# A raw memory projection with its norm applied at eviction, and head norms in column and row tiles of TensorE

## The reference

```python
def rmsnorm(x, g):
    y = x * lax.rsqrt(jnp.mean(x * x, axis=-1, keepdims=True) + EPS)
    return y * g

def memory_kv(mem, mem_norm_g, w_k, w_v, k_g):          # mem: 256 tokens x 2048
    mn = rmsnorm(mem, mem_norm_g)
    k = rmsnorm((mn @ w_k).reshape(B, N_MEM, MEM_H, MEM_HD), k_g)
    v = (mn @ w_v).reshape(B, N_MEM, MEM_H, MEM_HD)

# in layer(): xn = rmsnorm(x, norm1_g); one projection xn @ w_in gives the convolution, q, k, v, memory queries, gates
q = rmsnorm(qkv[:, :, :, 0], sw_q_g) * (SW_HD ** -0.5)   # 3 groups x 4 heads of 128
k = rmsnorm(qkv[:, :, :, 1], sw_k_g)
qm = rmsnorm(h_mq, mem_q_g) * (MEM_HD ** -0.5)           # 4 heads of 256
```

## Time and profile before

| | us |
|---|---|
| median of 3 runs | 3199.36 |
| lowest, highest | 3197.07, 3203.57 |
| the profiled execution | 3196.39 |
| its span (first to last instruction) | 3194.8 |
| PE busy in it | 3009.3 (94%) |
| DVE, ACT, POOL busy | 2007.6, 1361.9, 252.0 |

### The profile page before, as it was taken

One profiled execution on the slowest core, in us unless ns is written; L12 is line 12 of the kernel. 1 busy time (PEld: TensorE's weight loads), 2 busy tenths in 40 slices (PEclk: granted clock), 3 DMA queues, 4 the chain that ended last, 5 costly groups with the idle time before them and its releaser, 6 DMA issues.

```text
span 3194.8 us, 54045 instructions
## 1 busy us (share of the span) xinstructions
PE 3009.3 (94%) x21026; PEld 2777.8 (87%) x21026; DVE 2007.6 (63%) x2971; ACT 1361.9 (43%) x1825; POOL 252.0 (8%) x294
## 2 busy tenths in 40 slices
PE   5999998998868999999899999999999999999999
PEld 4899998866767998999899999999999887787777
DVE  4445886654323334643579986777774777787776
ACT  3343332344233333333334445777773443444444
POOL 1000001001000000100011101111100011011110
PEclk8999999989889999999999999999999999999999
DMA  4467778335654996867587878888887889999895
GB/s 163 164 224 279 275 266 207 116 114 182 232 208 159 392 369 255 310 241 260 193 296 272 280 280 289 309 331 307 328 315 265 310 331 334 335 339 331 329 329 186
DMA packets 227188, 854.95 MB, mean 268 GB/s; under 512 B 24768, under 2 KB 47312, under 8 KB 205104
## 3 DMA queue, kind: packets, MB, share of 16 engines
q1 hardware_dynamic: 182336, 563.68, 50.5%
q0 software_dynamic: 27088, 246.09, 21.6%
q10 hardware_dynamic: 17568, 42.48, 3.5%
HBM read 800.44 MB, written 139.26 MB: 294 GB/s over the span
## 4 chain that ended last, share of the span: by engine, by line
PE 75%; DMA 11%; DVE 8%; ACT 3%; issue 2%; DVEq 1%; SPq 0%; ACTq 0%; POOL 0%
PE ps L1546 19%; PE ps L1547 19%; PE ps L1548 19%; DMA raw<-in_v_rows 8%; PE ps L2028 3%; PE ps L2030 3%; PE ps L2029 3%; DVE w_lo L929 3%; PE ps L1993 2%; ACT w_hi L627 2%; DMA kv<-in_k_units 2%; DMA raw<-in_w_proj 1%; PE ps L1646 1%; PE ps L1718 1%; PE ps L1581 1%
## 5 line engine op out<-in xcount | busy, mean ns | idle before, releaser
L929 DVE TENSOR_TENSOR w_lo<-raw,w_hi 128x1024 fp32r<-128x1024 f32 x864 | 1057.4, 1225 | 950.7 <-ACT w_hi L627 944.3
L627 ACT ACTIVATE w_hi<-raw 128x1024 fp32r<-128x1024 f32 x864 | 912.2, 1058 | 1455.4 <-PE ps L1548 1077.8
L1546 PE MATMUL ps<-xs_hi,w_hi 128*128 128x320 f32 (+1 forms) x4672 | 1409.9, 302 | 46.2 <-ACT hb L669 12.4
L1547 PE MATMUL ps<-xs_lo,w_hi 128*128 128x320 f32 (+1 forms) x4672 | 1393.8, 298 | 0.0
L1548 PE MATMUL ps<-xs_hi,w_lo 128*128 128x320 f32 (+1 forms) x4672 | 1393.0, 298 | 0.0
L1546 PEld LDWEIGHTS ps<-xs_hi,w_hi 128*128 128x128 f32 x4672 | 893.0, 191 | 65.6 <-issue 44.2
L1547 PEld LDWEIGHTS ps<-xs_lo,w_hi 128*128 128x128 f32 x4672 | 893.3, 191 | 1.1
L1548 PEld LDWEIGHTS ps<-xs_hi,w_lo 128*128 128x128 f32 x4672 | 892.5, 191 | 0.0
L2028 PE MATMUL ps<-w_hi,cf_hi 128*128 128x512 f32 x1024 | 402.9, 393 | 15.8 <-DVE cf_lo L1499 15.8
L2030 PE MATMUL ps<-w_hi,cf_lo 128*128 128x512 f32 x1024 | 403.5, 394 | 0.0
L2029 PE MATMUL ps<-w_lo,cf_hi 128*128 128x512 f32 x1024 | 403.0, 394 | 0.0
(11 more groups left out here) (295 smaller groups left out, 1888.1 us busy)
## 6 DMA issues: line engine op xcount, KB each, us to landing
raw<-in_w_u SPq DMA_DIRECT2D x256, 512.0 KB, 4.6
raw<-in_v_rows SPq DMA_DIRECT2D x256, 512.0 KB, 6.9
raw<-in_w_gate_oproj SPq DMA_DIRECT2D x136, 512.0 KB, 5.9
raw<-in_w_proj SPq DMA_DIRECT2D x120, 512.0 KB, 4.9
o_sw_k<-in_sw_k POOLq DMA_DIRECT2D x32, 1020.0 KB, 7.5
o_sw_v<-in_sw_v POOLq DMA_DIRECT2D x32, 1020.0 KB, 7.3
kv<-in_k_units SPq DMA_DIRECT2D x104, 256.0 KB, 7.1
kv<-in_v_units SPq DMA_DIRECT2D x104, 256.0 KB, 7.1
```

Of the source, the lines that this page charges most:

```text
L627: A(w_hi[:, s, :], raw[:, s, :], ACT.Copy).then_inc(hi_done, 1)
L929: TT(w_lo[:, s, :], raw[:, s, :], w_hi[:, s, :].bitcast(F32), ALU.subtract).then_inc(lo_done, 1)
L1546: pe.matmul(out, a_hi, b_hi, start=start, stop=False)
L1547: pe.matmul(out, a_hi, b_lo, start=False, stop=False)
```

## The change

Two edits. In the memory stages the input is projected before its norm is known: `m_raw` times the gain is split into `mx_hi` and `mx_lo` by quarters as they arrive (ACT with a scale per partition, DVE with a fused multiply and subtract), and the norm's factor per token is multiplied in when a key tile leaves PSUM (`keep_key`) or, turned into a column by two transposes, when values leave it. The squares and their sums run between the key tiles, those of x as well, and x's scaling and splitting go beside the key and value stages. The loops of ACT, DVE and PE over these stages are written out, four banks take the key tiles, the parameters are loaded by ACT's queue, and POOL loads the convolution's state behind the value stage. In the head norms the four sums go to four column tiles of 32 columns each (every head's sum stands on 32 rows), and the spread takes them from four row tiles of 32 rows (`from_row` has a one in each tile's first row).

```diff
@@ SP
-            sp.dma_start(m_raw[:], a["memT"]).then_inc(m_loaded, 16)
+            for c in range(4):
+                sp.dma_start(m_raw[:, 4 * c:4 * c + 4, :], a["memT"][:, 4 * c:4 * c + 4, :]).then_inc(m_loaded[c], 16)
+                if c in (0, 2):
+                    load(a["w_memk"], c // 2, Place(MEMK0 + c // 2))
+            for r in range(2, 4):
+                load(a["w_memk"], r, Place(MEMK0 + r))
             sp.dma_start(x_raw[:], a["xT"]).then_inc(x_loaded, 16)
@@ POOL, ahead of the loads of the convolution's state
+            pool.wait_ge(w_released, MEMV0 + MEMV_BLOCKS)
@@ ACT
+            def memory_hi(c):
+                act.wait_ge(m_loaded[c], 16)
+                for k in range(4 * c, 4 * c + 4):
+                    last = A(mx_hi[:, k, :], m_raw[:, k, :], ACT.Identity, scale=gm[:, k:k + 1])
+                last.then_inc(m_hi_done, 1)
+            act.dma_start(prm[:], a["params"]).then_inc(prm_loaded, 16)
...
+            memory_hi(0)
+            split_hi(Place(0))
+            memory_hi(1)
+            split_hi(Place(1))
+            memory_hi(2)
+            memory_hi(3)
+            split_hi(Place(2))
+            split_hi(Place(3))
+            for t in range(MEMK_BLOCKS // 2):
+                if t < 2:
+                    square(2 * t, m_raw, NM)
+                    square(2 * t + 1, m_raw, NM)
+                if t == 2:
+                    act.wait_ge(sq_summed, 4)
+                    A(rms_m[:, 0, :], ps[:, 2, 0:NM], ACT.Sqrt, bias=EPS, scale=1.0 / D).then_inc(m_root, 1)
+                split_hi(Place(2 * t + 4))
+                if t in (2, 4):
+                    if t == 2:
+                        act.wait_ge(x_loaded, 16)
+                    square(t + 2, x_raw, NT)
+                    square(t + 3, x_raw, NT)
+                if t == 6:
+                    act.wait_ge(sq_summed, 8)
+                    A(rms_x[:, 0, :], ps[:, 3, 0:NT], ACT.Sqrt, bias=EPS, scale=1.0 / D).then_inc(rooted, 2)
+                split_hi(Place(2 * t + 5))
+            for r in range(MEMV_BLOCKS):
+                split_hi(Place(MEMV0 + 4 + r))
...
@@ DVE (memory_lo follows memory_hi quarter by quarter)
+            def keep_key(t):
+                ended(Place(MEMK0 + 2 * t + 1))
+                TT(mk[:, t, :], ps[:, (0, 1, 6, 7)[t % 4], 0:NM], rms_m[:, 1, :], ALU.mult).then_inc(bank_free, 1)
+            for t in range(MEMK_BLOCKS // 2):
+                split_lo(Place(2 * t + 4))
+                if t == 2:
+                    dve.wait_ge(m_root, 1)
+                    dve.reciprocal(rms_m[:, 1, :], rms_m[:, 0, :]).then_inc(m_root, 1)
+                    dve.drain()
+                    keep_key(0)
+                    keep_key(1)
+                if t == 6:
+                    dve.wait_ge(rooted, 2)
+                    dve.reciprocal(rms_x[:, 1, :], rms_x[:, 0, :])
+                    dve.drain()
+                    scale_by_norm(x_raw, x_raw, g1, rms_x, NT, 0, 6)
+                split_lo(Place(2 * t + 5))
...
@@ PE
+            for t in range(MEMK_BLOCKS // 2):
...
+                    if t == 0:
+                        pe.wait_ge(m_lo_done, 2 * half + 2)
+                    stream(n, ps[:, (0, 1, 6, 7)[t % 4], 0:NM], mx_hi, mx_lo, 8 * half, half == 0, half == 1, NM
+                           ).then_inc(w_released, 1)
+                if t < 2:
+                    sum_squares(2 * t, 2, NM)
+                    sum_squares(2 * t + 1, 2, NM)
+                if t == 2:
+                    pe.wait_ge(m_root, 2)
+                    pe.wait_ge(const_loaded, 16 * 4)
+                    for tt in range(2):
+                        last = pe.transpose(ps[:, 5, tt * P:(tt + 1) * P], rms_m[:, 1, tt * P:(tt + 1) * P], ident[:])
+                    last.then_inc(r_turned_m, 1)
+                if t in (3, 5):
+                    sum_squares(t + 1, 3, NT)
+                    sum_squares(t + 2, 3, NT)
@@ PE, head norms
-                    last = pe.matmul(ps[0:HG, 2, 0:NT], to_row[:, row, :], qk_sq[:, t, :], start=t == 0,
-                                     stop=t == HG - 1)
+                    last = pe.matmul(ps[32 * head:32 * head + 32, 2, 0:NT], ones[:, 0:32], qk_sq[:, t, :],
+                                     start=first, stop=final, tile_position=(0, 32 * head))
...
-                    last = pe.matmul(ps[:, 3 + t, 0:NT], from_row[:, t, :], r_row[:], start=True, stop=True)
+                    part = slice(32 * t, 32 * t + 32)
+                    last = pe.matmul(ps[:, 3 + t, 0:NT], from_row[part, :], r_row[part, :], start=True, stop=True,
+                                     tile_position=(32 * t, 0))
```

More of the change, by code:

```diff
@@ L627, in split_hi @@
                 A(w_hi[:, s, :], raw[:, s, :], ACT.Copy).then_inc(hi_done, 1)
-            def width_norm(src, cols, k, sq, root, bank):
-                for c in range(4):
-                    if c:
-                        act.wait_ge(sq_summed, 4 * k + c)
-                    A(sq[:, :, 0:cols], src[:, 4 * c:4 * c + 4, :], ACT.Square).then_inc(sq_done, 1)
-                act.wait_ge(sq_summed, 4 * k + 4)
-                A(root[:, 0, 0:cols], ps[:, bank, 0:cols], ACT.Sqrt, bias=EPS, scale=1.0 / D).then_inc(rooted, 1)
@@ L951, in _ @@
-            dve.wait_ge(xs_hi_done, 1)
-            TT(xs_lo[:, :, 0:NM], m_raw[:], xs_hi[:, :, 0:NM].bitcast(F32), ALU.subtract).then_inc(xs_lo_done, 1)
-            for n in range(4):
-                split_lo(Place(n))
-            dve.wait_ge(rooted, 2)
-            dve.reciprocal(rms_x[:, 1, :], rms_x[:, 0, :])
-            dve.drain()
-            scale_by_norm(x_raw, x_raw, g1, rms_x, NT, 0, KT).then_inc(normed, 1)
-            with dve.Fori(0, MEMK_BLOCKS // 4) as i:
-                for j in range(2):
-                    n = Place(MEMK0 + 2 * j, (4, i))
-                    split_lo(n + 4)
-                    split_lo(n + 5)
-                    ended(n + 1)
-                    move(tile_view(mk, i * 2 + j, 0, NM), ps[:, j, 0:NM]).then_inc(bank_free, 1)
@@ L968, in _ @@
-            with dve.Fori(0, 2) as i:
-                n = Place(MEMV0, (8, i))
-                for r in range(8):
-                    split_lo(n + (r + 4))
-                ended(n + 7)
-                move(mv[:, :, bass.ds(i * 512, 512)], ps[:, 0:2, :]).then_inc(bank_free, 2)
-            for half, ready, done in ((slice(0, 8), (x_hi_half, 1), x_lo_half),
-                                      (slice(8, 16), (xs_hi_done, 2), xs_lo_done)):
-                dve.wait_ge(*ready)
-                TT(xs_lo[:, half, :], x_raw[:, half, :], xs_hi[:, half, :].bitcast(F32), ALU.subtract
-                   ).then_inc(done, 1)
+            dve.wait_ge(prm_loaded, 16)
@@ new lines, in memory_lo @@
+            def memory_lo(c):
+                dve.wait_ge(m_hi_done, c + 1)
+                for k in range(4 * c, 4 * c + 4):
+                    last = STT(out=mx_lo[:, k, :], in0=m_raw[:, k, :], scalar=gm[:, k:k + 1],
+                               in1=mx_hi[:, k, :].bitcast(F32), op0=ALU.mult, op1=ALU.subtract)
+                last.then_inc(m_lo_done, 1)
+            def keep_key(t):
+                ended(Place(MEMK0 + 2 * t + 1))
+                TT(mk[:, t, :], ps[:, (0, 1, 6, 7)[t % 4], 0:NM], rms_m[:, 1, :], ALU.mult).then_inc(bank_free, 1)
@@ new lines, in _ @@
+            for r in range(MEMV_BLOCKS):
+                split_lo(Place(MEMV0 + 4 + r))
+                if r in (3, 6):
+                    half, ready, done = ((slice(0, 8), (x_hi_half, 1), x_lo_half),
+                                         (slice(8, 16), (xs_hi_done, 2), xs_lo_done))[r // 6]
+                    dve.wait_ge(*ready)
+                    TT(xs_lo[:, half, :], x_raw[:, half, :], xs_hi[:, half, :].bitcast(F32), ALU.subtract
+                       ).then_inc(done, 1)
+                if r % 8 == 7:
+                    i = r // 8
+                    ended(Place(MEMV0 + r))
+                    dve.drain()
+                    for tt in range(2):
+                        TS(mv[:, tt, 512 * i:512 * (i + 1)], ps[:, tt, :], rms_col[:, tt:tt + 1], None, ALU.mult
+                           ).then_inc(bank_free, 1)
```

120 lines of the change are left out of this document (68 added, 52 removed).

## The result

| | before, us | after, us | ratio, 95% interval |
|---|---|---|---|
| first comparison, median | 3198.22 (4 runs) | 3154.35 (4 runs, 3143.32 to 3159.40) | 0.9857 [0.9832, 0.9883] |
| second comparison (`after_again`), median | 3196.43 (11 runs) | 3139.89 (5 runs, 3133.98 to 3150.17) | 0.9827 [0.9808, 0.9845] |
| profiled execution, span (first) | 3194.8 | 3153.0 | |
| profiled execution, span (second) | 3178.1 | 3135.5 | |

The change is faster by 44 us in the first comparison and by 57 in the second; 59 were forecast. The first time, 3154, lies in the forecast range and 14 over the forecast of 3140; the second, 3140, lies on it. The question is where the 15 us of the first comparison are.

The account below looks back on a forecast made before the run. PE was taken as the bound, with 75% of the span. Gains of 29 us in the memory stages and 30 in the head norms sum to 59: 3137.4 us profiled, 3140 against the median, range 3128 to 3162.

Parts of the forecast that it names:

- Start: Memory stages: first projection matmul at 11.6 us instead of 56.76, after the first quarter lands at 5.3; block 1 at 17.2.
- Key stage: Memory keys: 15 blocks, sums of squares, transposes and one stall end at 78.0 instead of 104.9, 26.9 us gained.
- the stall for the reciprocal: Key stage: PE waits for DVE's reciprocal after blocks 4 and 5, 7.2 us against 5.8 of blocks, costing 1.4 us.
- Value stage: Memory values: waits of 3.3 ahead, 0.2 more in the middle, 3.8 instead of 6.55 last; memory part gains 29 us.
- rival (c): Startup quicker (3135 us) or slower (3145 us); forecast with either side of this had chance 0.70.
- Moved loads: Eight convolution-state loads moved behind the value stage stop nobody: cost taken as 0, bounds 0 and 12 us.
- Rival (b): Moved convolution-state loads hold up weight loads as the stores do: 15 us lost, 3155 us; chance 0.09.
- Head norms: Head-norm stage: column-tiled sums and row-tiled spreads, round 8.65 us, stage end at 728.2 instead of 758, 30 us gained.
- The drain at a change of mode: Head-norm tiles: shape changes taken at 0.1 us each; draining at 0.16 would make the sum 1.5 us worse.
- Rival (a): Head-norm spreads: row tiles don't overlap, 11 us lost, 3151 us; chance 0.12.
- Rival (d): Granted clock: PE stays at 1.2 GHz through key and value stages, 43 us slower than before, 3242 us; chance 0.04.
- Everything moves along.: Behind both parts, loads, copies and GpSimd's steps wait for tiles or norms, so they move along; no loss counted.

Follow-up runs that it names:

- after_again: The changed kernel unchanged, executed a second time under the profiler; 3139.89 us, ratio 0.9827.
- e4_order: Changed kernel with ACT's table loaded early, value evictions ahead of a split and x's second half subtracted four blocks later; 3137.9 us, ratio 0.9823.
- e10_shift: Changed kernel with 128 increments of an unused semaphore at the head of PE's queue; 3141.2 us, ratio 0.9837.
- e9_banks: Kernel of e4_order with the values' second half in two other PSUM banks, PE's loop written out, x's second half subtracted two blocks earlier; 3113.8 us, ratio 0.9745.
- e7_pieces: Kernel before with the memory input loaded in four pieces instead of one, nothing else; 3203.5 us (one run).
- e1_heads: Kernel before with only the head norms in column and row tiles, old memory stages kept; 3165.5 us, ratio 0.9904.
- before_again: The kernel before unchanged, executed a second time under the profiler; 3179.8 us (one run).

## Why the prediction was right, and where it was off

The two parts came out nearly as worked out, in places by errors that offset one another; the closing step behind them did not.

**Start.** Forecast 11.6, measured 13.51. The landing was taken at 5.3 and was 5.87; the quarter of scaled copies at 1.4 and was 1.70, the subtractions at 1.6 and 1.67. Not in the sum was ACT's table load of 1.28, which stands behind the wait for the first quarter; in the kernel before it came at 1.07, ahead of the wait. About half of this reached block 1. It was forecast to wait for quarter 3 until 17.2; in the run quarter 3 was done at 17.7, and PE, 24 matmuls after 13.51, came to block 1 only at 18.17:

```profile
18.17 0.28 PE L1610 MATMUL ps<-mx_hi,w_hi 128*128 128x256 f32 x1
```

**Key stage.** Forecast end 78.0, measured 78.0, to the tenth by luck: the start of block 1 was 1.0 us late, and the terms behind it were as much too long. Sums of squares 15.5 (twice 3.45 and twice 4.31) against 15.7, the stall for the reciprocal 1.3 against 1.4, and for the 15 blocks that leaves 42.6 against 43.2.

**Value stage.** This is the term that was mis-sized. The wait ahead of it was 3.47 (forecast 3.3) and the last one 4.35 (forecast 3.8); but the one in its middle, to which I gave 0.2 more than the 3.6 of before, was 5.55. I had the split of x covered by three split blocks, which holds for PE's operands; that the eviction stands behind it in DVE's own queue I had not counted. `e4_order` shows it: other places in that queue, and 5.55 becomes 1.68. The part gave 26.1 us instead of 29, and 24.1 between the two repeats; rival (c), an earlier or later start, was not what decided it. The middle wait before (PE's waits):

```profile
PE ps L1546 <- DVE mv L923: 3.6, 1, 3.6
```

**Moved loads.** Taken at 0, measured at 0. They are issued from 136 to 143 us and land 4.2 to 5.7 us later; the two weight loads among them take 3.6 and 5.2 us, PE waits for no weight load there (its 4.35 us at 140.42 end with DVE's eviction), and the store of the convolution's state behind the projection still holds a weight load for 29.3 us. Rival (b) is out.

**Head norms.** Forecast 30, measured 30.1 (103.4 less 73.3, from the first sum at 629.54 to the end of the last spread at 702.8). Spread 0.75 (0.7), sum 0.68 and 1.21 (0.6 and 1.2), round 8.66 (8.65), the first round ended by DVE 10.8 us into the stage (10.8). That the round fits to 0.01 is luck in part. It holds 8.66 - 0.75 - 0.68 = 7.23 beside spread and sum, where a gate of 7.05 and 0.3 of changes were taken. A round of before holds as much with the old shapes: its sum ends at 721.33 + 3.94 = 725.27, its next spread is

```profile
732.50 2.35 PE ps L1655 x8
```

and lies 7.23 later. So the gate was taken 0.18 too short, the changes 0.3 too long and the small matmuls 0.13 too short; the tiles' changes of shape cost nothing visible that the old shapes did not. The drain at a change of mode that the Trainium skill, TensorEngine Tiling (Array Packing), Key Properties, states was weighed as 0.16 a change, 0.48 a round; the trace leaves 0.18 a round for it at most, and has the same 0.18 without these tiles. Row tiles are 2.9 times as fast as four full matmuls of 2.15 and 3.1 times as fast as the old spread of 2.35. The Trainium skill, TensorE: Matmul & The Clock Gate, Part 3, has 3.07 for four tiles of 32 rows at 512 columns, and the trace, at 320, agrees. Rival (a) is out.

**The clock.** Rival (d) is out as a whole: it was 1.00 from about 18 us to the end of the key stage. But it fell to 0.5 for a few microseconds behind each of the three waits of 3.47, 5.55 and 4.35 (0.63, 0.50 and 0.55 in the rows above), as it had behind the old ones in the first trace of before, and this goes into the 26.1.

**"Everything moves along."** This step failed. It says that stages that are not touched keep their length. The attention stage took 6.5 us more (0.2% of the time), reproducibly. A change of the length of PE's program ahead of it takes this back (457.0 in `e10_shift`, 458.3 in `e9_banks`); since `e7_pieces` loses 4 us without any such change, it is not shown that this length alone is the cause, and the path from it to the loads of keys stays open. The last weight stage took 6.3 us more in the first comparison, which is chance: it was 14 us shorter in the next execution. With 2.9 us from the value stage and 0.9 in the input projection (from its start to the layer norm's sums 450.3 before, 451.1 after, but 448.0 in `after_again`: chance too) these are 16.6 of the 17.3 us by which the first profiled execution, 3154.71, missed its forecast of 3137.4. The second comparison gains 56.5 of the forecast 59 although attention lost as much in its trace; so its agreement is in part luck: the last stage scatters by enough to make up for that, and medians do not tell more.

## What to carry to other kernels

Ahead of a wait, list the whole queue of the engine that ends it: an eviction stands behind every split and subtraction issued before it, and another order in that queue and then two spare banks brought the next stage forward by 9 us each here. Small matmuls, of few columns or few rows, gained here by going to tiles of the array side by side: of the 30 us, the overlap made 19 and the clock that no longer fell 8 to 11. When two numbers agree to a tenth, compare their terms too: the key stage and the round of the head norms agreed by errors that offset. When a total misses a forecast by 0.5%, compare stage by stage over several executions before looking for a cause: one stage here scatters by 20 us whatever the kernel.

## What had not been expected of the hardware

The length of PE's program ahead of a stage can change that stage: 128 semaphore increments moved the attention stage by -8.3 us in one kernel and by +6.6 in another, with PE's waits for the same loads at 25.5 instead of 37.3 and 33.4 instead of 29.7. Idle time of 1.68 and 1.95 us left the granted clock at 1.00, while behind 3.47, 4.35 and 5.55 us it was 0.63, 0.55 and 0.50 in the rows above. The 2.82 us ahead of the old value stage did either: behind them the clock was 0.50 in the first trace of before and stayed at 1.00 in its repeat, which has the same wait of 2.82 (as in `e1_heads`; in `e7_pieces` it fell). Busy time behind the wait, in before and in `before_again`:

```profile
108.00:112.00 4.00, 4.00 (x10) 3.13 (x11) 0.00 (x0) 0.00 (x0) 0.00 (x0) 0.50 0.36 131
```

```profile
109.00:113.00 4.00, 3.96 (x17) 3.30 (x18) 0.00 (x0) 0.91 (x1) 0.00 (x0) 1.00 0.37 131
```

In 4 us PE does 10 matmuls in the one and 17 in the other. So a gain that hangs on the clock behind one such wait needs more than one trace. One stage of 740 us, bound by PE and the loads of weights together, took from 728.7 to 749.3 us in 14 executions, at an idle time of PE between 9 and 23 us in the two traces of the changed kernel.
